# Sparse attention of an encoder block: table loads moved behind the sixth unit, choice rounds in units 1 to 4, head scaling in units 9 to 12, two logit banks instead of three

## What is computed

```
hm = head_rms_norm(mlstm(...), g_mlstm_head)      # 4 heads x 128, 512 tokens
hm = sigmoid(mo) * hm
# sparse attention: 4 query heads x 128, one shared key and value head
score -> top 128 admissible keys per token -> mask
logits = q . k * scale, masked;  p = softmax(logits);  ha = p . v
y = concat(hm, ha) @ w_out                        # next stage
```

## Time and profile before

| | before |
|---|---|
| median of 3 runs | 1054.93 us (1053.38 to 1056.37) |
| profiled execution, its own time | 1055.45 us |
| its span in the trace | 1053.6 us |
| PE / DVE / ACT busy share of the span | 94% / 87% / 65% |
| stage_attention in the trace | 200.8 to about 274.1 us |
| the 16 units: first mask to last copy_out | 234.14 to 274.07 us |
| output projection begins | 274.39 us |
| ScalarE busy, of that table loads at L865 and L875 | 684.6 us, 1.28 us each |

### The profile page before, as it was taken

One profiled execution on the slowest core, in us unless ns is written; L12 is line 12 of the kernel. 1 busy time (PEld: TensorE's weight loads), 2 busy tenths in 40 slices (PEclk: granted clock), 3 DMA queues, 4 the chain that ended last, 5 costly groups with the idle time before them and its releaser, 6 DMA issues.

```text
span 1053.6 us, 15339 instructions
## 1 busy us (share of the span) xinstructions
PE 988.6 (94%) x5065; PEld 780.7 (74%) x5066; DVE 912.1 (87%) x1266; ACT 684.6 (65%) x742; POOL 202.9 (19%) x144
## 2 busy tenths in 40 slices
PE   0899999978999999999999999999999999999986
PEld 0898889756546547888888888878878878878874
DVE  3888899878576747999999999999999999999984
ACT  2524365465222137888888888888888888888862
POOL 0000000100000031222322322322334233333310
PEclk9899999998999999999999999999999999999998
DMA  9776210330594539999999999999999999999932
GB/s 353 284 256 227 83 42 1 118 143 1 197 376 154 205 111 373 349 374 378 380 374 385 367 374 366 374 366 381 366 371 360 380 367 382 377 378 379 315 85 96
DMA packets 89333, 296.25 MB, mean 281 GB/s; under 512 B 17185, under 2 KB 29645, under 8 KB 79821
## 3 DMA queue, kind: packets, MB, share of 16 engines
q1 hardware_dynamic: 69476, 259.18, 63.6%
q0 software_dynamic: 18304, 33.60, 13.0%
q10 hardware_dynamic: 1514, 2.97, 0.8%
HBM read 289.39 MB, written 39.32 MB: 312 GB/s over the span
## 4 chain that ended last, share of the span: by engine, by line
PE 40%; DVE 12%; issue 10%; ACT 2%; DVEq 0%
PE ps L2099 23%; PE ps L2157 9%; PE ps L2089 4%; DVE w_down_lo L1968 3%; DVE xT_lo L1950 2%; DVE w_gate_up_lo L1946 2%; ACT w_gate_up_hi L1816 2%; PE ps L2117 2%; DVE pick L1928 1%; PE ps L2107 1%; DVE uT_lo L1959 1%; DVE u L1955 1%; PE ps L2175 0%; DVE pad L1602 0%; DVE xt L2073 0%
## 5 line engine op out<-in xcount | busy, mean ns | idle before, releaser
L1946 DVE TENSOR_TENSOR w_gate_up_lo<-side,w_gate_up_hi 128x2048 fp32r<-128x2048 f32 x64 | 146.3, 2286 | 11.7 <-ACT w_gate_up_hi L1816 9.3
L1613 POOL DMA_INDIRECT y_rows<-yb,row_numbers x62 | 120.9, 1950 | 184.3 <-DMA y_rows<-yb,row_numbers 124.3
L1946 DVE TENSOR_TENSOR w_gate_up_lo<-main,w_gate_up_hi 128x2048 fp32r<-128x2048 f32 x64 | 146.4, 2288 | 5.4 <-ACT w_gate_up_hi L1816 3.4
L2099 PE MATMUL ps<-w_gate_up_hi,xT_hi 128*128 128x512 f32 x512 | 144.4, 404 | 6.1 <-DVE xT_lo L1950 5.2
L2099 PE MATMUL ps<-w_gate_up_hi,xT_lo 128*128 128x512 f32 x512 | 137.5, 390 | 0.0
L2099 PE MATMUL ps<-w_gate_up_lo,xT_hi 128*128 128x512 f32 x512 | 137.0, 389 | 0.0
L1816 ACT ACTIVATE w_gate_up_hi<-side 128x2048 fp32r<-128x2048 f32 x64 | 122.3, 1912 | 5.7 <-PE ps L2099 3.7
L1816 ACT ACTIVATE w_gate_up_hi<-main 128x2048 fp32r<-128x2048 f32 x64 | 122.5, 1914 | 2.6 <-PE ps L2099 2.3
L2099 PEld LDWEIGHTS ps<-w_gate_up_hi,xT_hi 128*128 128x128 f32 x512 | 91.2, 188 | 29.0 <-issue 12.5
L2099 PEld LDWEIGHTS ps<-w_gate_up_hi,xT_lo 128*128 128x128 f32 x512 | 96.1, 188 | 21.0
L2099 PEld LDWEIGHTS ps<-w_gate_up_lo,xT_hi 128*128 128x128 f32 x512 | 96.1, 188 | 20.4
(11 more groups left out here) (319 smaller groups left out, 1808.9 us busy)
## 6 DMA issues: line engine op xcount, KB each, us to landing
side<-in_w_exp_gate SPq DMA_DIRECT2D x60, 512.0 KB
side<-in_w_exp_up SPq DMA_DIRECT2D x60, 512.0 KB
main<-in_w_exp_gate SPq DMA_DIRECT2D x60, 512.0 KB
main<-in_w_exp_up SPq DMA_DIRECT2D x60, 512.0 KB
side<-in_w_ada SPq DMA_DIRECT2D x20, 1024.0 KB, 7.7
main<-in_w_exp_down SPq DMA_DIRECT2D x16, 1024.0 KB
maskb<-in_w_exp_down SPq DMA_DIRECT2D x16, 1024.0 KB
side<-in_w_exp_down SPq DMA_DIRECT2D x16, 1024.0 KB
```

The lines of the kernel that those rows point to most:

```text
L1613: return pool.indirect_dma_start(out=G.y_sums, out_offset=bass.IndirectOffsetOnAxis(ap=sidx[:, n:n + 1], axis=0), in_=yb[:, slot, :], in_o ...
L1946: nc.vector.tensor_tensor(wlo[:, half], src, whi[:, half].bitcast(F32), ALU.subtract).then_inc(s_wlo, 1)
L2099: ins = nc.tensor.matmul(ps[0:CAP, 2 + slot, :], xp[:, HALF * half + c, :], wp[:, half, c].rearrange("p m f -> p (m f)"), start=half == 0 ...
```

## The change

ScalarE loads the exp table with a small extra Exp ahead of the units; head 3's squares move to unit 1, the square root behind unit 5's exp and copy, copy_head to units 10 to 13, and copy_out comes over from VectorE. VectorE makes the variances in unit 3, runs the choice rounds in units 1 to 4 and the head scaling in units 9 to 12. TensorE does turn(u) ahead of logits(u + 2), and logits alternate between banks 0 and 1; the transposed heads take bank 2 in units 9 to 12.

```diff
-        rsum = sb("rsum", [P, 2])
+        rsum = sb("rsum", [P, 3])
-        LAST_ROUNDS = (5, 6, 7, 8)
+        LAST_ROUNDS = (1, 2, 3, 4)
+        HEADS_AT = 8
+        ROOT_AT = 5
 # ScalarE
-            for h in range(2, HEADS):
-                head_squares(h)
-            act.wait_ge(s_hsq, 1)
-            nc.scalar.activation(rstd[:, :, :], var[:, :, :], ACT.Sqrt).then_inc(s_hrt, 1)
+            head_squares(2)
+            nc.scalar.activation(rsum[:, 2:3], k[:, K_ONES:K_ONES + 1], ACT.Exp)
             act.wait_ge(s_num, HEADS)
...
             for u in range(len(UNITS)):
                 exp_unit(u)
                 if u:
                     copy_pT(u - 1)
-                if 2 <= u < HEADS + 2:
-                    copy_head(u - 2)
+                if u == 1:
+                    head_squares(3)
+                if u == ROOT_AT:
+                    act.wait_ge(s_hsq, 1)
+                    nc.scalar.activation(rstd[:, :, :], var[:, :, :], ACT.Sqrt).then_inc(s_hrt, 1)
+                if 2 <= u - HEADS_AT < HEADS + 2:
+                    copy_head(u - HEADS_AT - 2)
+                if u >= HEADS + 2 and (u - 2) % HEADS == 0:
+                    copy_out((u - 2) // HEADS - 1)
             copy_pT(len(UNITS) - 1)
+            copy_out(NT - 1)
 # VectorE
-            dve.wait_ge(s_vsq, HEADS)
-            nc.vector.tensor_scalar(var[:, :, :], var[:, :, :], 1.0 / DH, EPS, ALU.mult, ALU.add).then_inc(s_hsq, 1)
...
             for u in range(len(UNITS)):
                 mask_unit(u)
-                if 1 <= u <= HEADS:
-                    norm_head(u - 1)
+                if u == 3:
+                    dve.wait_ge(s_vsq, HEADS)
+                    nc.vector.tensor_scalar(var[:, :, :], var[:, :, :], 1.0 / DH, EPS, ALU.mult, ALU.add).then_inc(s_hsq, 1)
+                if 1 <= u - HEADS_AT <= HEADS:
+                    norm_head(u - HEADS_AT - 1)
                 if u:
                     invert(u - 1)
                 if u in LAST_ROUNDS:
...
-                if u >= HEADS + 2 and (u - 2) % HEADS == 0:
-                    copy_out((u - 2) // HEADS - 1)
             invert(len(UNITS) - 1)
-            copy_out(NT - 1)
 # TensorE
             def logits(u):
                 h, i = UNITS[u]
-                if u >= 3:
-                    pe.wait_ge(s_lgd, u - 2)
-                nc.tensor.matmul(ps[:, u % 3, ...
+                if u >= 2:
+                    pe.wait_ge(s_lgd, u - 1)
+                nc.tensor.matmul(ps[:, u % 2, ...
...
             for u in range(len(UNITS)):
+                turn(u)
                 if u + 2 < len(UNITS):
                     logits(u + 2)
-                turn(u)
                 if u:
                     attend(u - 1)
-                if 1 <= u <= HEADS:
-                    turn_head(u - 1)
+                if 1 <= u - HEADS_AT <= HEADS:
+                    turn_head(u - HEADS_AT - 1)
```

More of the change, by code:

```diff
@@ L883, in copy_pT, with copy_out @@
                 nc.scalar.activation(prT[:, u % 2, 0:w], ps[:, 3 + u % 3, 0:w], ACT.Copy).then_inc(s_pTd, 1)
+            def copy_out(i):
+                act.wait_ge(s_o, HEADS * (i + 1))
+                nc.scalar.activation(catT[:, HEADS:2 * HEADS, i * P:(i + 1) * P],
+                                     ps[:, 6 + i % 2, :].rearrange("p (h t) -> p h t", h=HEADS), ACT.Copy).then_inc(s_od, 1)
             def copy_head(h):
                 act.wait_ge(s_hT, h + 1)
-                nc.scalar.activation(catT[:, h, :], ps[:, 7, :], ACT.Copy, scale=cols[:, 40 + h:41 + h]).then_inc(s_hTd, 1)
+                nc.scalar.activation(catT[:, h, :], ps[:, 2, :], ACT.Copy, scale=cols[:, 40 + h:41 + h]).then_inc(s_hTd, 1)
             for u in range(len(UNITS)):
@@ L986, in mask_unit @@
                     dve.wait_ge(s_ex, u - 1)
-                nc.vector.tensor_tensor_reduce(out=lg[:, u % 2, 0:w], in0=ps[:, u % 3, 0:w], in1=maskb[:, i, 0:w], scale=-SCALE,
+                nc.vector.tensor_tensor_reduce(out=lg[:, u % 2, 0:w], in0=ps[:, u % 2, 0:w], in1=maskb[:, i, 0:w], scale=-SCALE,
                                                scalar=-FMIN, op0=ALU.add, op1=ALU.min,
@@ L1077, in turn_head @@
                 for i in range(NT):
-                    ins = nc.tensor.transpose(ps[:, 7, i * P:(i + 1) * P], hall[:, i, h * DH:(h + 1) * DH], ident)
+                    ins = nc.tensor.transpose(ps[:, 2, i * P:(i + 1) * P], hall[:, i, h * DH:(h + 1) * DH], ident)
                 ins.then_inc(s_hT, 1)
@@ L1082, in logits @@
                 h, i = UNITS[u]
-                if u >= 3:
-                    pe.wait_ge(s_lgd, u - 2)
-                nc.tensor.matmul(ps[:, u % 3, 0:P * (i + 1)].rearrange("p (j t) -> p j t", t=P), nat[:, i, AQ0 + h * DH:AQ0 + (h + 1) * DH],
+                if u >= 2:
+                    pe.wait_ge(s_lgd, u - 1)
+                nc.tensor.matmul(ps[:, u % 2, 0:P * (i + 1)].rearrange("p (j t) -> p j t", t=P), nat[:, i, AQ0 + h * DH:AQ0 + (h + 1) * DH],
                                  nat[:, 0:i + 1, AK0:AK0 + DH], start=True, stop=True).then_inc(s_lg, 1)
@@ L1100, in attend @@
                 pe.wait_ge(s_pTd, u + 1)
-                if i == 1 and h == 0:
-                    pe.wait_ge(s_hTd, HEADS)
                 if i >= 2 and h == 0:
```

## The result

The changed kernel took **1066.82 us** in the median of 4 runs (1065.31 to 1102.62), the kernel before 1054.99: ratio 1.011, 95% interval 1.0091 to 1.013. It is slower, as forecast, but by 11.8 us and not 7.8, and 0.8 us above the top of the range. The profiled execution took 1065.31 us, span 1063.4: 9.9 us over the one of before.

The account below looks back on a forecast made before the run. TensorE was taken to bound the units from 248 us to the barrier; turn(15) 7.8 us later (278.2 against 270.44) on 1055.45 gave 1063.2, less 0.5 to the median 1062.8. Own range 1061 to 1065, stated range 1058 to 1066.

Parts of the forecast that it names:

- part 1: Start: early exp load brings unit 0's exp to 233.4 us, 3.5 us earlier; its reciprocal, R(0), starts at 233.9.
- part 2: Units 0 to 5: clock low from about 236 to 247 us; reciprocals R(2) at 238.3, R(4) at 243.4.
- my upper bound: Unit 6's reciprocal, R(6), at latest 249.1 us, set by mask(7) at the low clock.
- rival B: Units 6 to 9: clock stays or falls low, 3 to 4 steps about 1.1 us longer; 1066.5 us, chance 0.08.
- part 3: Behind unit 5: load, root, load take 2.82 us; exp(6) at 248.3, R(6) at 248.9, 1.5 of 3.5 us left.
- rival D: Mid-loop table switches cost more than their loads, as long again for each of two; 1065.4 us, chance 0.02.
- part 4: Order on TensorE: turn, logits, mask, invert form a chain in each unit; turn(15) at 278.2 us, 7.8 us later.
- the eight steps: Full-clock steps between reciprocals from R(6) to R(14): 2.42, 3.76, 3.69 twice, 4.02, 2.97, 3.19 twice; sum 26.9 us.
- own range: Whole kernel 1061 to 1065 us: R(6) from 247.8 to 249.1, late clock 1 us more, 0.1 error per step.
- A: Units 7 to 13: TensorE stays the bound, not slower; turn(15) at 269.2 us, total 1053.7, chance 0.13.
- C: Units 9 to 12: head scaling lies outside the chain, four times 1.05 us less; 1058.6 us, chance 0.03.
- E: Start: the one-column Exp doesn't bring the table load forward, 1.3 us later there; 1064 us, no chance of its own.

Follow-up runs that it names:

- e5: Changed kernel plus products nobody reads: three of 512 columns behind logits(1), one of 384 behind attend(u - 1) in the first units; 1062.43 us, ratio 1.0049.
- e2: Changed kernel with logits(u + 2) put back ahead of turn(u); 1052.64 us, ratio 0.997.
- e4: Kernel before the change with only turn(u) put ahead of logits(u + 2); 1064.28 us, ratio 1.0077.
- e3: Changed kernel with the head scaling behind invert(u - 1) instead of ahead of it; 1060.35 us, ratio 1.004.
- e1: The changed kernel again, unaltered, for more executions; 1066.54 us in the median of 11, ratio 1.0094.
- e9: Changed kernel plus only the three products of 512 columns that nobody reads, behind logits(1); 1064.72 us, ratio 1.0086.
- e8: e6 with the square root behind unit 4's exp and copy instead of unit 5's; 1051.73 us, ratio 0.9968.
- e6: Changed kernel with logits ahead of turn (e2) and the head scaling behind invert (e3) together; 1052.99 us, ratio 0.996.

## Why the prediction was wrong in size and right in kind

- **The start, part 1.** Right. First exp 1.24 us after the last head's row began, forecast 1.4; R(0) 1.75 us after it, forecast 1.9.
- **Units 0 to 5, part 2.** Right up to R(4) (11.43 us after the last head, forecast 11.4), then 0.6 us short: R(6) came after 17.52 us (forecast 248.9 - 232.02 = 16.9). What gated R(6) was mask(7) behind its logits (249.64, a wait of 2.17 us), not the root's loads, by which it would have come at 17.05 (exp(6) at 248.92, and 0.6). That is the case of my upper bound, 249.1 or 17.1, and the bound was itself short: a turn of two key tiles takes 1.01 us at the low clock (0.97 in rival B's terms), and with two such steps behind R(4) my own terms give 249.3. In e5, at full clock, R(6) waits for exp(6) again.
- **The root, part 3.** Right in its cost: 2.82 us, with nothing added to either load (rival D falls). Before the change the squares ahead of it end at 234.02, and not at 233.84 as I read; the sum starts at 234.04 and doesn't hang on it. Of the 3.5 us won at the start 0.84 were left at R(6), forecast 1.5.
- **The order, part 4.** Right. e2 takes the chain away and the loss with it, e4 makes it on the kernel before, e3 takes the scaling out of it, e5 shows the eight steps as worked out. The turn of unit 9 took 0.77 to the next product, as I had kept it, and its weight load began with it at 261.53, not ahead. The Trainium skill ("TensorE: Matmul & The Clock Gate", "Step-by-step: what each phase is for") has weight loads pulled ahead of running matmuls. No matmul was running in that wait, so the row doesn't contradict the page; it shows only that the load didn't go ahead of its own turn's wait.
- **What failed** is the term "I take the clock as low from about 236 to 247" in part 2 (and R(6) gated by the root, which hangs on it), and the own range built on it ("1 us more if the clock comes back only in unit 8"). It was low to 253.4 in one trace, and from 257 to 263.8 a second time in the other (e1). In the first that is 0.6 us at R(6) and 1.14 in the step to R(7), 1.8 of the 1.9 us by which turn(15) missed (48.08 against 278.2 - 232.02 = 46.2). In the second, the two long steps alone are 1.98 us more than 3.69 each. e5, with the clock held, has the forecast's steps and is 4.1 us faster by the medians. That this equals the miss (1066.82 - 1062.8 = 4.0) is in part luck: e5 also gives back 1.1 us of low clock that the forecast had counted (248.9 against 247.8). By its trace the profiled execution missed by 2.1 us (1065.31 against 1063.2), and the clock is 1.8 of that. The other two stood 1.4 to 1.6 us above it, and how much of this is clock no trace shows; in e1's trace, 1.9 us longer than the first, it is 0.9. By e1's ratio the whole miss is 2 us (1.0094 against 1.0074).
- I gave B a chance of 0.08 with the argument that the clock had stayed through a wait of 1.05 us. That wait was one; the chain has one of 1.0 to 1.95 us ahead of every turn from turn(8) to turn(11). The clock fell behind them in e1 and e9, and stayed in the first trace and in e5, with the same waits. So B was less a rival than something that the likeliest case brings in some executions. Its total, 1066.5, came near the measured one by luck: it had put 3 to 4 slow steps in units 6 to 9, and the first trace has one.
- Rivals A and C fell by the traces: the wait ahead of the masks is 1.68 us and not 1.1, and the head scaling stands between mask and reciprocal (259.94 to 261.00; e3 takes it out). A's sum with logits in time, turn(15) at 269.2 or 37.2 us after the last head, is about what e2 gave (36.83). E fell too: the load stands at 232.31, ahead of unit 0's exp. The first comparison's 11.8 us and the second's 10.9 differ by what executions differ; the profiled execution, 9.9 us, was the shortest of its four.

## What to carry to other kernels

In an engine's hand-written order, an instruction that feeds the next unit belongs ahead of one that waits for the present unit; put behind, it closes a chain through all engines in every unit, and its length is the sum of the parts whatever the busy shares say. When costing such a chain, cost TensorE's clock with it: waits in every unit make sparse work, sparse work can bring the lower level (two of four traces here in units 9 and 10), and that level lengthens the chain again. A table load in a loop is worth placing beside work that another engine has of its own: in e8 against e6 that brought turn(15) forward by 1.6 us, though the times don't tell it.

## What the runs showed of the hardware

The same steps on TensorE brought the clock down in one execution and not in another (busy 4.34 of the 6.9 us ahead of the fall in e1; 4.15 of 7.0 us without a fall in the first trace, 253.4 to 260.4), so one trace is a poor bound for it. Products that nobody reads held it up in the two traces that have them in the units: 7 of 384 and 3 of 512 columns made a kernel about 4 us faster where it had a chain, and bought nothing where it had none. Two loads of function tables in mid loop cost 2.82 us with the root between them, the same as ahead of the loop.
